# Up-projections of the attention latents as three products of rounded parts

## The reference, cut to what matters

```
cq   = rmsnorm(h @ w_dq, q_norm)                 # 256 tokens x 512
q    = einsum('btc,chd->bthd', cq, w_uq)         # 16 heads x 96
ckv  = rmsnorm((h @ w_dkv)[:, :256], kv_norm)    # new tokens x 256
ckv_all = concatenate([cache_ckv, ckv_s])        # latent tokens read 128 cached rows too
k_nope = einsum('bsc,chd->bshd', ckv, w_uk)      # 16 heads x 64
v      = einsum('bsc,chd->bshd', ckv, w_uv)      # 16 heads x 64
```

## Time and profile before

| | |
|---|---|
| median of three runs | 1638.74 us |
| the profiled execution | 1639.95 us, its span 1638.1 us |
| PE busy in the span | 1592.0 us (97%) |
| DVE, ACT busy | 1159.3 us (71%), 976.0 us (60%) |
| DMA | 498.27 MB, 304 GB/s on the mean |
| up-projections, from the first `uq` to the last `uv` product | 63.88 to 117.33 us of the span |

### The profile page before, as it was taken

How to read it: one execution, slowest core, us unless ns; L and a number is a source line. 1 busy time by engine, 2 the same in 40 slices (tenths; PEclk the granted TensorE clock), 3 DMA queues, 4 the chain that set the end, 5 groups by cost and what they waited for, 6 DMA issues and landing times.

```text
span 1638.1 us, 23054 instructions
## 1 busy us (share of the span) xinstructions
PE 1592.0 (97%) x8975; PEld 1324.4 (81%) x8975; DVE 1159.3 (71%) x1082; ACT 976.0 (60%) x972; POOL 39.4 (2%) x39
## 2 busy tenths in 40 slices
PE   7999999999999989999999999999999999999997
PEld 5755799899789879788888888888888888888886
DVE  1245344443764674788888888888888888988988
ACT  1135244333673545767777777777777767767774
POOL 0000000000000010000000000000000000000001
PEclk9998999999899999899999999999999999999999
DMA  9748359757358017799999999999999999999994
GB/s 363 275 169 328 103 209 352 262 206 266 139 199 295 21 47 235 265 379 386 371 381 378 368 388 374 371 384 371 380 377 366 388 381 368 378 372 365 380 377 148
DMA packets 201347, 498.27 MB, mean 304 GB/s; under 512 B 8592, under 2 KB 12223, under 8 KB 186943
## 3 DMA queue, kind: packets, MB, share of 16 engines
q1 hardware_dynamic: 194030, 477.96, 79.1%
q0 software_dynamic: 3984, 14.17, 2.5%
q10 hardware_dynamic: 3264, 5.19, 0.8%
HBM read 485.60 MB, written 11.69 MB: 304 GB/s over the span
## 4 chain that ended last, share of the span: by engine, by line
PE 52%; DVE 5%; issue 4%; ACT 2%; DVEq 0%; ACTq 0%
PE banks L711 50%; DVE weights_low L2043 2%; ACT weights_high L1572 2%; PE banks L1207 1%; DVE hidden_low L2145 1%; DVE tokens_low L2056 1%; DVE arena L2141 0%; PE banks L1176 0%; PE banks L1146 0%; DVE ring L1991 0%; ACT arena L1686 0%; DVE arena L2219 0%; DVE arena L2186 0%; ACT L1608 0%; ACT L1321 0%
## 5 line engine op out<-in xcount | busy, mean ns | idle before, releaser
L2043 DVE TENSOR_TENSOR weights_low<-pieces,weights_high 128x2048 fp32r<-128x2048 f32 x336 | 754.0, 2285 | 131.0 <-ACT weights_high L1572 131.0
L1572 ACT CAST weights_high<-pieces 128x2048 fp32r<-128x2048 f32 x336 | 624.9, 1913 | 31.1 <-PE banks L711 25.1
L711 PE MATMUL banks<-weights_high,tokens_high 128*128 128x512 f32 x896 | 354.6, 396 | 0.7 <-DVE tokens_low L2056 0.7
L711 PE MATMUL banks<-weights_low,tokens_high 128*128 128x512 f32 x896 | 350.1, 391 | 0.0
L711 PE MATMUL banks<-weights_high,tokens_low 128*128 128x512 f32 x896 | 348.8, 389 | 0.0
L711 PEld LDWEIGHTS banks<-weights_low,tokens_high 128*128 128x128 f32 x896 | 168.2, 188 | 35.9
L711 PEld LDWEIGHTS banks<-weights_high,tokens_high 128*128 128x128 f32 x896 | 168.9, 188 | 33.7 <-issue 0.8
L711 PEld LDWEIGHTS banks<-weights_high,tokens_low 128*128 128x128 f32 x896 | 168.6, 188 | 33.5
L711 PE MATMUL banks<-weights_high,hidden_high 128*128 128x512 f32 x448 | 175.9, 393 | 2.9 <-DVE hidden_low L2145 2.9
L711 PE MATMUL banks<-weights_low,hidden_high 128*128 128x512 f32 x448 | 174.7, 390 | 0.0
L711 PE MATMUL banks<-weights_high,hidden_low 128*128 128x512 f32 x448 | 174.4, 389 | 0.0
(11 more groups left out here) (256 smaller groups left out, 2090.7 us busy)
## 6 DMA issues: line engine op xcount, KB each, us to landing
pieces<-in_moe_w SPq DMA_DIRECT2D x336, 1024.0 KB, 7.6
ring<-in_w_ada SPq DMA_DIRECT2D x24, 2048.0 KB, 10.9
ring<-in_ffn_w SPq DMA_DIRECT2D x15, 2048.0 KB, 11.6
ring<-in_hg_w_f SPq DMA_DIRECT2D x4, 2048.0 KB, 19.0
expert_rows<-arena POOLq DMA_DIRECT2D x9, 512.0 KB, 7.2
ring<-in_mla_w_o SPq DMA_DIRECT2D x2, 2048.0 KB, 8.9
ring<-in_hg_w_i SPq DMA_DIRECT2D x2, 2048.0 KB, 7.8
ring<-in_hg_w_q SPq DMA_DIRECT2D x2, 2048.0 KB, 8.5
```

Of the source, the lines that this page charges most:

```text
L711: return pe.matmul(o_, lhsT=l, rhs=r, start=start, stop=stop, skip_group_check=True)
L1572: act.copy(parts_hi[:, p % PARTS, :], raw[:, p % RAW, :]).then_inc(rounded, 1)
L2043: dve.tensor_tensor(parts_lo[:, p % PARTS, :], raw[:, p % RAW, :], parts_hi[:, p % PARTS, :].bitcast(F32), ALU.subtract).then_inc(split, 1)
```

## The change

Four "high" blocks are added to the list of weights, one behind each of `uq` (two halves), `uk` and `uv`, and each of these blocks is split into a high part (ScalarE, `round_latent`) and a low part (VectorE, `split_latent`, written over the block itself). The two latents are split as well: `cq_hi`, `cq_lo` and `ckv_hi`, `ckv_lo`. TensorE waits for the split weights (`up_split`) in place of the landing, and makes three products for each of before. The counts of later semaphores shift by four blocks and six latent pieces.

```
-        for j in range(2):
-            add(("uq", j), kmaj(uq, slice(8 * QK * j, 8 * QK * (j + 1))))
-        add(("uk",), ...)
-        add(("uv",), ...)
+        LATENT = [("uq", 0), ("uq", 1), ("uk",), ("uv",)]
...
+        for name, src in zip(LATENT, latent_src):
+            add(name, src)
+            blocks.append((("high",) + name, None))
...
# TensorE
-            pe.wait_ge(nout, 1)
+            def latent_weights(b):
+                pe.wait_ge(up_split, b + 1)
+                return latent_place(b)[1:]
             for h2 in range(HEADS // 2):
                 if h2 % 4 == 0:
-                    w = have(pe, ("uq", h2 // 4))
+                    w = latent_weights(h2 // 4)
...
-                    last = chunk_product(bank[h2 % 4][0:QK, T * m:T * m + T], w, slice(QK * c, QK * c + QK), cqT, QL // P)
+                    for k in range(QL // P):
+                        if h2 == m == 0:
+                            pe.wait_ge(x_split, k + 1)
+                        last = products(bank[h2 % 4][0:QK, T * m:T * m + T], [t[:, k, QK * c:QK * c + QK] for t in w],
+                                        (cq_hi[:, k, :], cq_lo[:, k, :]), k == 0, k == QL // P - 1)
...
-                    last = mm(bank[h2 % 4][:, 0:KEYS], w[:, k, 2 * NOPE * h2:2 * NOPE * (h2 + 1)], ckvT[:, k, :], k == 0, k == 1)
+                    if h2 == 0:
+                        pe.wait_ge(x_split, KV_BEFORE + k + 1)
+                    last = products(bank[h2 % 4][:, 0:KEYS], [t[:, k, 2 * NOPE * h2:2 * NOPE * (h2 + 1)] for t in w],
+                                    (ckv_hi[:, k, :], ckv_lo[:, k, :]), k == 0, k == 1)
...
-                    last = mm(bank[j % 4][:, :], ckvT[:, k, P * t:P * t + P], w[:, k, 512 * half:512 * half + 512], k == 0, k == 1)
+                    last = products(bank[j % 4][:, :], [x[:, k, P * t:P * t + P] for x in (ckv_hi, ckv_lo)],
+                                    [x[:, k, 512 * half:512 * half + 512] for x in w], k == 0, k == 1)
# ScalarE
+            def round_latent(b):
+                whole, high, _ = latent_place(b)
+                have(act, LATENT[b])
+                act.wait_ge(*spent(number[("high",) + LATENT[b]] - RING))
+                act.copy(high, whole).then_inc(up_rounded, 1)
+            round_latent(0)
             act.wait_ge(kv_taken, 2)
             squares(1, cq_sq, cqT)
             root(1, QL)
+            for c in range(QL // P):
+                act.wait_ge(nout, c + 1)
+                act.copy(cq_hi[:, c, :], cqT[:, c, :]).then_inc(x_high, 1)
             act.wait_ge(kv_taken, 3)
             squares(2, ckv_sq, ckvT[:, :, 0:T])
+            round_latent(1)
             for h2 in range(HEADS // 2):
...
+                if h2 == 1:
+                    round_latent(2)
                 if h2 == 3:
                     root(2, KVL)
+                if h2 == 5:
+                    for c in range(KVL // P):
+                        act.wait_ge(nout, KV_BEFORE + c + 1)
+                        act.copy(ckv_hi[:, c, :], ckvT[:, c, :]).then_inc(x_high, 1)
+                    round_latent(3)
# VectorE
+            def split_latent(b):
+                whole, high, rest = latent_place(b)
+                dve.wait_ge(up_rounded, b + 1)
+                dve.tensor_tensor(rest, whole, high.bitcast(F32), ALU.subtract).then_inc(up_split, 1)
+            split_latent(0)                  # before the copies of the query latent
...
             for c in range(QL // P):
-                last = dve.scalar_tensor_tensor(cqT[:, c, :], ...)
-            last.then_inc(nout, 1)
+                dve.scalar_tensor_tensor(cqT[:, c, :], ...).then_inc(nout, 1)
+            for c in range(QL // P):
+                dve.wait_ge(x_high, c + 1)
+                dve.tensor_tensor(cq_lo[:, c, :], cqT[:, c, :], cq_hi[:, c, :].bitcast(F32), ALU.subtract).then_inc(x_split, 1)
...
+            split_latent(1)                  # behind the copies of the cached rows
+            split_latent(2)
...
+            for c in range(KVL // P):        # behind the two scalings of the key latent
+                dve.wait_ge(x_high, KV_BEFORE + c + 1)
+                dve.tensor_tensor(ckv_lo[:, c, :], ckvT[:, c, :], ckv_hi[:, c, :].bitcast(F32), ALU.subtract).then_inc(x_split, 1)
+            split_latent(3)
```

More of the change, by code:

```diff
@@ L209, in hybrid_step @@
         assert lo <= RING * SLOT + ARENA
+        cq_hi = x_hi[:, 0:QL // P, :]
+        cq_lo, _ = rounded_tensor("latent_query_low", RING * SLOT + HEADS * (T + KEYS), (QL // P, T))
+        ckv_hi, lo = rounded_tensor("latent_key_high", RING * SLOT + oT_end + KVL // P * KEYS, (KVL // P, KEYS))
+        ckv_lo, _ = rounded_tensor("latent_key_low", lo, (KVL // P, KEYS))
         silu_g = hT[:, 0:2, :]
@@ L426, in hybrid_step @@
         uq = a["mla_w_uq"][0].rearrange("c h d -> c (h d)")
-        for j in range(2):
-            add(("uq", j), kmaj(uq, slice(8 * QK * j, 8 * QK * (j + 1))))
-        add(("uk",), kmaj(a["mla_w_uk"][0].rearrange("c h d -> c (h d)"), slice(0, HEADS * NOPE)))
-        add(("uv",), kmaj(a["mla_w_uv"][0].rearrange("c h d -> c (h d)"), slice(0, HEADS * VD)))
+        LATENT = [("uq", 0), ("uq", 1), ("uk",), ("uv",)]
+        latent_src = [kmaj(uq, slice(8 * QK * j, 8 * QK * (j + 1))) for j in range(2)]
+        for name, n in (("mla_w_uk", HEADS * NOPE), ("mla_w_uv", HEADS * VD)):
+            latent_src.append(kmaj(a[name][0].rearrange("c h d -> c (h d)"), slice(0, n)))
+        for name, src in zip(LATENT, latent_src):
+            add(name, src)
+            blocks.append((("high",) + name, None))
         add_ada(*range(4, 10))
@@ L468, in spent @@
                 f_end = sum(c for _, c in ffn_blocks[:at[0] + 1]) // P
-                return (down_split, f_end) if kind == "w2" else (up_split, 2 * f_end - (kind == "w1"))
+                return (down_split, f_end) if kind == "w2" else (up_split, len(LATENT) + 2 * f_end - (kind == "w1"))
             j = at[0] if at else 0
@@ L521, in hybrid_step @@
         assert [ring_slot(number[h + ("o", j)]) for j in range(2) for h in ((), ("high",))] == [3, 6, 4, 5]
-        MIXER_FROM = 2 * (D_FF // P)
+        MIXER_FROM = len(LATENT) + 2 * (D_FF // P)
         def mixer_place(b):
@@ L528, in mixer_place, with latent_place @@
             return slot(n, DC, 512), high, rest
+        def latent_place(b):
+            n, n_high = number[LATENT[b]], number[("high",) + LATENT[b]]
+            _, k, cols = blocks[n][1].shape
+            high, rest = (ring_rounded[ring_slot(m)][:, 0:k * cols].rearrange("p (k n) -> p k n", k=k) for m in (n_high, n))
+            return slot(n, k, cols), high, rest
         def mixer_piece(h):
@@ L551, in hybrid_step @@
         SCALED_BEFORE = (0, DC, 2 * DC, 4 * DC)
-        HIGH_BEFORE = (None, 0, DC)
-        O_BEFORE = 3 * DC
+        KV_BEFORE = QL // P
+        HIGH_BEFORE = (None, KV_BEFORE + KVL // P, KV_BEFORE + KVL // P + DC)
+        O_BEFORE = HIGH_BEFORE[1] + 3 * DC
         INPUTS_BEFORE = (0, None, None, DC)
@@ L855, in rotations @@
                     mm(dst, con("rot", QK), src, True, True).then_inc(rot_ready, 1)
-            pe.wait_ge(nout, 2)
-            w = have(pe, ("uk",))
+            w = latent_weights(2)
             for h2 in range(HEADS // 2):
@@ L868, in _ @@
                     rotations()
-            w = have(pe, ("uv",))
+            w = latent_weights(3)
             for j in range(6):
@@ L956, in _ @@
                 for half in range(2):
-                    pe.wait_ge(up_split, 2 * f + half + 1)
+                    pe.wait_ge(up_split, len(LATENT) + 2 * f + half + 1)
                     w = [dense_part(t, f, half) for t in (dense_hi, dense_lo)]
@@ L1721, in modulated_norm @@
                         shift = mod[:, 0, DC * SHIFT_FFN + c - 1, :]
-                        dve.wait_ge(x_high, c)
+                        dve.wait_ge(x_high, HIGH_BEFORE[1] + c)
                         for g in range(G):
@@ L1794, in _ @@
             for c in range(QL // P):
-                last = dve.scalar_tensor_tensor(cqT[:, c, :], cqT[:, c, :], cols_b[:, R_QN + c:R_QN + c + 1],
-                                                norm_bank[1][:, T:2 * T], ALU.mult, ALU.mult)
-            last.then_inc(nout, 1)
+                dve.scalar_tensor_tensor(cqT[:, c, :], cqT[:, c, :], cols_b[:, R_QN + c:R_QN + c + 1],
+                                         norm_bank[1][:, T:2 * T], ALU.mult, ALU.mult).then_inc(nout, 1)
+            for c in range(QL // P):
+                dve.wait_ge(x_high, c + 1)
+                dve.tensor_tensor(cq_lo[:, c, :], cqT[:, c, :], cq_hi[:, c, :].bitcast(F32), ALU.subtract).then_inc(x_split, 1)
             dve.wait_ge(cq_ready, 4)
@@ L1805, in _ @@
             for c in range(KVL // P):
-                last = dve.scalar_tensor_tensor(ckvT[:, c, 0:T], ckvT[:, c, 0:T], cols_b[:, R_KVN + c:R_KVN + c + 1], rstd,
-                                                ALU.mult, ALU.mult)
-            last.then_inc(nout, 1)
```

(6 more changed lines are left out.)

4 lines of the change are left out of this document (2 added, 2 removed).

## The result

The changed kernel takes 1625.53 us (median of four runs, 1624.62 to 1628.27), the kernel before in the same comparison 1638.77 us (1636.62 to 1639.06): a ratio of 0.992, 95% interval 0.9903 to 0.9937. The forecast was 1630.5 us, with a range of 1626.5 to 1635.0. The gain was 13.2 us where 8.2 were predicted, so the time lies 1 us under the range. The profiled execution took 1624.62 us, its span 1622.5 against 1638.1: 15.6 us apart.

What follows compares the result with a forecast made beforehand. TensorE, busy all the time at full clock, was taken to bound the up-projections. Terms -4.6 - 2.0 - 2.15 + 0.55 = -8.2 us took 1638.74 to 1630.5 us, range 1626.5 to 1635.0.

Steps and rivals of the forecast that it cites:

- The sum: Up-projections: `uq` -4.6, `uk` -2.0, `uv` -2.15 and a later start +0.55, together -8.2 us.
- 24 products at 0.12 us: One `uq` step after the change: 2.88 us instead of 3.45, so eight steps save 4.6 us.
- the middle of the two bounds: `uk` products of 384 columns: 0.173 us each, between 0.12 and 0.225; eight steps save 2.0 us.
- The late start: Before `uq`: TensorE waits for the query latent's first low part and is then paced for three pieces, cost 0.55 us.
- The cover: Up-projections: the new casts and subtractions hide in waits of ScalarE and VectorE, 0.55 us excepted.
- the line through two sizes: Cast and subtraction times at 256 and 2048 elements, extended to half of `uq`: 2.77 us on ScalarE, 3.35 on VectorE.
- the splits were not on the path: Rival: TensorE waits for split weights in `uq`, `uk` and `uv`, up to 20.6 us, whole 1651; chance 0.04.
- ScalarE did not hold `uk`: Rival: ScalarE's copies keep the `uk` step at 1.29 us, 2.0 us lost, whole 1632.5; chance 0.10.
- products did not overlap more: Rival: up-projection products run closer together, by the skill page's spacing, another 3.4 us, whole 1627.1; chance 0.03.
- The loads: SyncE's loads: six ada blocks start later as ring slots come free, yet land before they are wanted; cost nothing.
- the span after that as long as before: Sign to check: from the attention's first ada product, near 111.4, onward, the program takes as long as before.
- the clock falls: Rival: another half-clock stretch in the up-projections, or a longer one in attention, costs 2.7 to 6.8 us; chance 0.08.

Runs made afterwards that it cites:

- the second and third comparison: Kernel before, unaltered, timed beside the changed kernel again, filler and `uq` alone (1638.64 us), then beside kernels with 2, 6, 3 and 7 unused products (1639.12 us).

## Why the prediction was wrong, by its own steps

- **The sum held.** A step of `uq` is 2.81 us on the mean of the first three where 2.88 were due: eight save 5.1 us, predicted 4.6. The size that was off is 24 products at 0.12 us, a rounded distance; they start 0.117 us apart. `uk` goes from 1.29 to 1.04 (2.0 us, as predicted; the middle of the two bounds was right), `uv` from 1.71 to 1.36 (2.1, predicted 2.15). The late start is 0.42 us (0.47 less the 0.05 of before), predicted 0.55, since nothing but the first low part is waited for long. Together -8.8 by these terms, -8.75 from the scalings to the first ada product, predicted -8.2.
- **The cover held.** The first half is cast at 47.33 (predicted 47.2) in 2.74 us and its rest takes 3.36 (2.77 and 3.35 from the line through two sizes). TensorE's 24.10 us of `uq` have no idle time at the splits, so the splits were not on the path; ScalarE did not hold `uk`, 0.1 us of cover was enough; six products in 1.36 us of `uv` are 0.227 us each, so products did not overlap more. On this spacing the Trainium skill's page "TensorE: Matmul & The Clock Gate", section "Back-to-back issue gap", gives 131 ns for 512 columns, and the trace does not agree.
- **The loads held.** The six ada blocks start at 76.00, `wo` at 109.22, and the first ada product stands at 111.09 with no wait (predicted 76, 109 and 111.4).
- **The step that failed** is the one from the sum to the forecast: "1638.74 - 8.2 = 1630.5 us", with its mark "the span after that as long as before". It took everything behind the attention as fixed. It is not: over the traces that part lasts 0.37 us longer for each us that TensorE spends in it at half clock, and it took from 1475.4 to 1486.0 us. In the profiled executions the kernel before stood at 47.8 us of half clock and the changed one at 27.3, and 7.55 us came from there. The median moved 5 us more than the forecast. Of this, 0.55 us are the sum (8.75 against 8.2) and some 2 us the half-clock time that the runs have on record (56.6 against 51.0 us on the mean); the other 2 us or so stay open. The rival "the clock falls" saw the mechanism, had its 13.6 us and priced it as a loss only, 2.7 to 6.8 us. The same rows held a gain: if that one stretch went away, 2.0 us in the attention and 2.4 in `wo` (30.30 less the 27.89 measured at full clock, not the 2.7 of the prediction) would go with it, 4.4 in all as measured since, and the range should have reached to 1630.5 - 4.4 = 1626.1, or further with the routing's 2.3 us.
- **What is shown and what is open.** Shown: the traces' length behind the attention follows the half-clock time on one line for both kernels; the same products take longer in these stretches; the changed kernel's advantage runs from 0.2 to 12.4 us with nothing altered but the position. Supported by the clocks on record, but not seen in traces: that the medians differ in part for the same reason. Open: the last 2 us or so of the gain; why a position meets more or fewer such stretches, and why they move between executions of one kernel.

## What to carry to other kernels

Price a shorter stage from the stage itself, and then ask what else in the program depends on where in time it stands: each stretch at half clock in the trace before is a term of either sign, a loss if there is one more and a gain if there is one less. To tell a change's own worth from such a shift, read it between two events close around the change, or time both kernels at several positions by adding a little unused work ahead of the change. Look at the granted clock of every run and not of the traced one alone: here the first trace of the changed kernel came from the run with the least half-clock time of ten. Where a gain is larger than the changed stage can hold, the rest comes from elsewhere and has to be looked for there.

## What was not expected of the hardware

The kernel before alone ran from 1632.55 to 1644.31 us over the second and third comparison (50 runs), wider than the whole gain predicted. Adding 1.7 us of unused products to it gave 1634.99 us against 1640.68 (ratio 0.9974, 0.995 to 0.9998). At full clock, fp32r products of 256 columns start 0.117 us apart (96 output rows, 2.81 / 24), of 384 columns 0.173 us (1.04 / 6) and of 512 columns 0.227 us (1.36 / 6).
